# A two-layer decoder trunk on one core: the side sum of the expert rows moves from VectorE to ScalarE and GpSimd

## The reference, cut to what matters

```python
# per block of 128 tokens, 8 heads, 16 picks a head = 128 picks a token
e = ...                      # index of each pick in a table of 16384 experts
g = softmax(sc)              # gate of each pick
ue = u[e]; ve = v[e]         # two rows of 1024 floats a pick and token
a = gelu(einsum('thkd,td->thk', ue, xb)) * g
out = einsum('thk,thkd->td', a, ve)
```

## Time and profile before

| | |
|---|---|
| median of three runs | 2906.79 us |
| time of the profiled execution | 2907.78 us |
| its span in the trace | 2906.0 us |
| busy: TensorE matmul / VectorE / ScalarE / GpSimd | 78% / 75% / 41% / 43% |
| granted TensorE clock, mean | 0.921 of full speed |
| moved by DMA | 1170.26 MB, mean 403 GB/s |

### The profile page before, as it was taken

The page is one execution under the profiler, slowest core; times in us unless marked ns, Lnnn a source line. Parts: engine busy times, 40 slices in busy tenths (PEclk is TensorE's granted clock), DMA queues, the critical chain, the costliest instruction groups (busy, mean ns, idle before and its releaser), DMA issues.

```text
span 2906.0 us, 27009 instructions
## 1 busy us (share of the span) xinstructions
PE 2257.9 (78%) x7300; PEld 1200.6 (41%) x7300; DVE 2185.6 (75%) x5166; ACT 1183.3 (41%) x3457; POOL 1263.8 (43%) x1049
## 2 busy tenths in 40 slices
PE   8678777687877877787787878878778777876667
PEld 6535443354423544243343434433444434432222
DVE  2687768875878757796688876988679876887664
ACT  2144324343443433344444463445534453433333
POOL 0155335443454433444434543354434454345555
PEclk9799899999998998899898998999899998998989
DMA  6499999999999999999999999999999999999998
GB/s 270 174 410 421 413 359 420 421 420 413 404 420 422 420 389 415 421 422 421 421 391 416 422 421 421 388 413 421 421 418 398 420 421 420 404 420 422 421 422 351
DMA packets 170816, 1170.26 MB, mean 403 GB/s; under 512 B 19668, under 2 KB 19928, under 8 KB 36136
## 3 DMA queue, kind: packets, MB, share of 16 engines
q0 software_dynamic: 147456, 1073.81, 89.4%
q1 hardware_dynamic: 23208, 94.74, 8.3%
HBM read 1164.28 MB, written 4.19 MB: 402 GB/s over the span
## 4 chain that ended last, share of the span: by engine, by line
DMA 29%; DVE 14%; PE 10%; issue 6%; POOL 3%; ACT 3%; POOLq 0%; DVEq 0%; ACTq 0%
DMA ring<-in_uv,pick 27%; PE acc L1716 5%; DVE ring L1093 5%; POOL ring L666 3%; PE ps L1511 3%; DVE side L1084 1%; DMA xc<-h 1%; DMA stream<-in_strips 1%; ACT diag L1369 1%; DVE arena L968 1%; DVE arena L949 1%; DVE arena L950 1%; ACT coef L1361 1%; DVE arena L1039 1%; DVE arena L1043 1%
## 5 line engine op out<-in xcount | busy, mean ns | idle before, releaser
L666 POOL DMA_INDIRECT ring<-in_uv,pick x1024 | 1259.3, 1230 | 1616.5 <-PE acc L1716 1084.1
L1716 PE MATMUL acc<-ring,diag 128*128 128x512 f32 x2988 | 1523.6, 652 | 474.6 <-ACT diag L1369 474.1
L1093 DVE CUSTOM_DVE_ANT_0 ring<-ring,h_now 128x1024 f32<-128x1024 f32 x1024 | 1236.0, 1223 | 494.5 <-DMA ring<-in_uv,pick 483.2
L1716 PEld LDWEIGHTS acc<-ring,diag 128*128 128x128 f32 x2988 | 576.0, 204 | 1286.0 <-ACT diag L1369 719.4
L1358 ACT ACTIVATE gelu<-dots 128x1 f32<-128x1 f32 x1024 | 206.1, 201 | 1263.2 <-DVE dots L1093 1261.8
L1084 DVE SCALAR_TENSOR_TENSOR side<-ring,coef,side 128x1024 f32<-128x1024 f32 x270 | 346.1, 1282 | 18.9 <-ACT coef L1361 18.9
L1361 ACT ACTIVATE coef<-gate,gelu 128x1 f32<-128x1 f32 x1024 | 301.9, 295 | 33.2
L1369 ACT ACTIVATE diag<-ident,coef 128x128 f32<-128x128 f32 x747 | 300.1, 402 | 28.2 <-PE acc L1716 3.9
L1511 PE MATMUL ps<-resident,actT 128*128 128x256 f32 x896 | 217.5, 399 | 16.5 <-ACT actT L1170 16.5
L1511 PEld LDWEIGHTS ps<-resident,actT 128*128 128x128 f32 x896 | 175.7, 200 | 59.4 <-ACT actT L1170 18.1
L1478 PE MATMUL ps<-actT,stream 128*128 128x128 f32 x960 | 125.6, 292 | 27.4 <-DMA stream<-in_strips 26.6
(11 more groups left out here) (196 smaller groups left out, 1439.2 us busy)
## 6 DMA issues: line engine op xcount, KB each, us to landing
stream<-in_strips SPq DMA_DIRECT2D x102, 512.0 KB, 9.3
resident<-in_strips SPq DMA_DIRECT2D x18, 1024.0 KB, 12.3
ring<-in_uv,pick POOLq DMA_INDIRECT x1024, 14.9
ring<-in_strips SPq DMA_DIRECT2D x9, 1024.0 KB, 19.7
arena<-in_keys SPq DMA_DIRECT2D x8, 512.0 KB, 7.8
xc<-in_x SPq DMA_DIRECT2D x4, 512.0 KB, 6.2
h<-arena SPq DMA_DIRECT2D x4, 512.0 KB, 11.5
xc<-h SPq DMA_DIRECT2D x4, 512.0 KB, 7.8
```

The lines of the kernel that those rows point to most:

```text
L666: pool.indirect_dma_start(ring[:, n % SLOTS, :], None, tables[layer], bass.IndirectOffsetOnAxis(ap=pick[:, col:col + 1], axis=0),).then_in ...
L1093: dve.tensor_tensor_reduce(ring[:, slot, 0:D], ring[:, slot, 0:D], h_now[:], 1.0, 0.0, ALU.mult, ALU.add, dots[:, slot:slot + 1]).then_inc ...
L1716: m = pe.matmul(acc[:, b * 512:(b + 1) * 512], diag[:, turn % 4, :], ring[:, slot, D + b * 512:D + (b + 1) * 512], start=(r == 0 and i == ...
```

## The change

The table `VECTOR` becomes `ADDED`, with more even rounds: 25 picks in the first stage, 35 in each gla stage, 33 in each swa stage, 260 in all; 764 picks go to TensorE. VectorE's instruction L1084 is gone. For a listed pick ScalarE, after `coef`, multiplies the v half by it in place. GpSimd adds the product to `side`, right before the gather that will reuse the slot, which is nine picks later in its order. That addition marks the slot used, and so it now also gives the signal for the load of `xc`.

```diff
-VECTOR = {
-    "first": (
-        ((),) * 2 + ((4,),) + ((),) + ((1, 4, 7),) + ((0, 2, 4, 6),) + ((1, 3, 5, 7),) * 2 +
-        ((0, 2, 4, 6),) * 3 + ((1, 4, 7),) + ((2, 6),) + ((),) * 3),
-    "gla": (
-        ((1, 4, 7),) * 3 + ((0, 2, 4, 6),) + ((1, 4, 7),) * 2 + ((0, 2, 4, 6),) + ((1, 3, 5, 7),) +
-        ((0, 3, 6),) + ((2, 6),) + ((1, 4),) + ((2, 6),) + ((4,),) + ((),) * 3),
-    "swa": (
-        ((1, 4, 7),) * 2 + ((0, 2, 4, 6),) + ((0, 4),) + ((1, 5),) + ((0, 3, 6),) + ((2, 6),) +
-        ((1, 4, 7),) * 2 + ((2, 6),) + ((1, 3, 5, 7),) + ((0, 3, 6),) + ((),) * 4),
+ADDED = {
+    "first": ((),) * 3 + ((2, 6),) + ((1, 4, 7),) * 7 + ((2, 6),) + ((),) * 4,
+    "gla": ((1, 4, 7),) * 11 + ((2, 6),) + ((),) * 4,
+    "swa": ((1, 4, 7),) * 11 + ((),) * 5,
 }
...
+            def add(n):
+                s, at = divmod(n, PICKS)
+                r, i = divmod(at, BATCH)
+                added = ADDED[kind_of(s)]
+                pool.wait_ge(multiplied, ADDED_PICKS.index(n) + 1)
+                began = True
+                if i != added[r][0]:
+                    released(pool, pick_number(s, r, added[r][added[r].index(i) - 1]))
...
+                else:
+                    began = False
+                    pool.wait_ge(side_folded, s + 1)
+                slot = n % SLOTS
+                pool.tensor_tensor(side[:], ring[:, slot, D:2 * D], (side if began else xc)[:],
+                                   ALU.add).then_inc(used[slot], 1)
+
             def gathers(s, layer, begin, end):
                 for i in range(begin, end):
                     n = s * PICKS + i
+                    if n >= SLOTS and n - SLOTS not in TURN_OF:
+                        add(n - SLOTS)
                     if n >= SLOTS:
                         released(pool, n - SLOTS)
...
-                    dve.scalar_tensor_tensor(side[:], ring[:, slot, D:2 * D], coef[:, slot:slot + 1],
-                                             (side if began else xc)[:], ALU.mult, ALU.add).then_inc(used[slot], 1)
...
                         act.activation(coef[:, slot:slot + 1], gate[:, col:col + 1], ACT.Copy,
                                        scale=gelu[:, slot:slot + 1]).then_inc(weighed, 1)
+                        act.wait_ge(weighed, n + 1)
                         if i not in tensor[r]:
+                            v = ring[:, slot, D:2 * D]
+                            act.activation(v, v, ACT.Copy, scale=coef[:, slot:slot + 1]).then_inc(multiplied, 1)
                             continue
-                        act.wait_ge(weighed, n + 1)
```

More of the change, by code:

```diff
@@ L58 @@
 BEATS = PICKS // BEAT
-VECTOR = {
-    "first": (
-        ((),) * 2 + ((4,),) + ((),) + ((1, 4, 7),) + ((0, 2, 4, 6),) + ((1, 3, 5, 7),) * 2 +
-        ((0, 2, 4, 6),) * 3 + ((1, 4, 7),) + ((2, 6),) + ((),) * 3),
-    "gla": (
-        ((1, 4, 7),) * 3 + ((0, 2, 4, 6),) + ((1, 4, 7),) * 2 + ((0, 2, 4, 6),) + ((1, 3, 5, 7),) +
-        ((0, 3, 6),) + ((2, 6),) + ((1, 4),) + ((2, 6),) + ((4,),) + ((),) * 3),
-    "swa": (
-        ((1, 4, 7),) * 2 + ((0, 2, 4, 6),) + ((0, 4),) + ((1, 5),) + ((0, 3, 6),) + ((2, 6),) +
-        ((1, 4, 7),) * 2 + ((2, 6),) + ((1, 3, 5, 7),) + ((0, 3, 6),) + ((),) * 4),
+ADDED = {
+    "first": ((),) * 3 + ((2, 6),) + ((1, 4, 7),) * 7 + ((2, 6),) + ((),) * 4,
+    "gla": ((1, 4, 7),) * 11 + ((2, 6),) + ((),) * 4,
+    "swa": ((1, 4, 7),) * 11 + ((),) * 5,
 }
-TENSOR = {kind: tuple(tuple(i for i in range(BATCH) if i not in v) for v in of) for kind, of in VECTOR.items()}
+TENSOR = {kind: tuple(tuple(i for i in range(BATCH) if i not in v) for v in of) for kind, of in ADDED.items()}
 FOLD_AT = 14
@@ L86 @@
 TURN_OF = {n: turn for turn, n in enumerate(TURNED)}
+ADDED_PICKS = [n for n in range(STAGES * PICKS) if n not in TURN_OF]
 AT = {
@@ L304, in build @@
         weighed = sem("weighed")
+        multiplied = sem("multiplied")
         diag_ready = sem("diag_ready")
@@ L494, in load_block @@
                 elif stage:
-                    released(sp, pick_number(stage - 1, 0, VECTOR[kind_of(stage - 1)][0][0]))
+                    released(sp, pick_number(stage - 1, 0, ADDED[kind_of(stage - 1)][0][0]))
                 if prep.layer == 1:
@@ L652, in stage @@
                     gathers(s, layer, begin, (part + 1) * PICKS // PARTS)
+            def add(n):
[6 more added lines that the diff above has]
+                    released(pool, pick_number(s, r, added[r][added[r].index(i) - 1]))
+                elif any(added[:r]):
+                    last = max(m for m in range(r) if added[m])
+                    released(pool, pick_number(s, last, added[last][-1]))
+                elif kind_of(s) == "first":
+                    pool.wait_ge(side_begun, 1)
+                else:
[4 more added lines that the diff above has]
+                                   ALU.add).then_inc(used[slot], 1)
             def gathers(s, layer, begin, end):
@@ L1094, in part @@
                                                  ALU.add, dots[:, slot:slot + 1]).then_inc(dotted, 1)
[L1095 to L1098, removed]
                 return part
@@ L1707, in part @@
                     if r == FOLD_AT and picks[0] == 0:
-                        fold(s, VECTOR[kind_of(s)])
+                        fold(s, ADDED[kind_of(s)])
                     for i in picks:
```

## The result

The changed kernel takes 3037.69 us (median of four runs, 3022.35 to 3044.55) against 2906.26 us: ratio 1.0445, 95% interval 1.0417 to 1.0473. It is 131 us slower where 43 were forecast. The profiled execution took 3034.2 us, its span 3032.5 us.

What follows compares the result with a forecast made beforehand. The prediction took the DMA engines' pace as the bound. To the profiled 2907.8 us it added 24 for GpSimd's unrefilled lead and 19 for the late xc load, 2951, or 2950 against the median; range 2898 to 3050.

Steps and rivals of the forecast that it cites:

- The bound: Whole kernel: it runs at the pace of the DMA engines, 420 to 422 GB/s in most slices.
- the direction: Whole kernel: slower with chance 0.76, same 0.12, faster 0.12.
- GpSimd's work: GpSimd's rounds with three additions take 21.2 us against 21.1; lead not refilled, 24 us lost over four swa stages.
- VectorE's additions go: VectorE: 277 instructions, 355 us less; costed at nothing, since its time is mostly cover; ceiling 29 us.
- unless its dots are stretched: Sign on VectorE: it loses 355 us of busy time, unless its dots take longer.
- rival B: GpSimd becomes the bound: additions and dots block each other in turn, a round takes 23.9 us; 3075 us, chance 0.14.
- the placement: TensorE: 17 more picks and their new distribution over rounds, 35 us more work; costed at 0, upper end 6 us in four stages.
- the multiplication: ScalarE: 260 multiplications, 276 us more, between coef and the addition; hidden by the lead, costed at 0.
- The load of xc: Turns of stages 3 to 6: the load starts 5.8 us later, 19 us lost; stages 1 and 2 at 0.
- A: Only the xc load costs, as cheap additions let the lead be won back before round 5; 2926 us, chance 0.20.
- D: No change: GpSimd's additions are hidden by the 17.3 us of lead everywhere; 2907 us, chance 0.12.
- C: Faster: VectorE's dots come earlier in crowded rounds and slices below 420 GB/s partly fill; 2885 us, chance 0.12.

Runs made afterwards that it cites:

- one_after: Changed kernel, but the dot reads one input and writes no product back (a reduction of about the same length): 2960.5 us, ratio 1.0188.
- write: Changed kernel, but GpSimd writes zeros over the slot and half of the side sum in place of adding, about the same GpSimd time without reading: 2990.19 us, 1.0283.
- first: Changed kernel, but the first addition of stages 1 to 7, which signals the load of xc, stays on VectorE: 3018.63 us, 1.0394.
- short: Changed kernel, but GpSimd adds only 8 of 1024 columns, with all waits and the order kept: 2920.88 us, 1.0050.
- mult: Kernel before with the new table of picks and the multiplication on ScalarE, the addition still on VectorE: 2919.67 us, 1.0051.
- sqlate: Kernel before, but in stages 3 to 6 the norm of the next block begins three picks later: 2907.57 us, 1.0002.
- pick0: Kernel before, but the first addition of each stage from the second on is of pick 0 instead of pick 1: 2908.69 us, 1.0005.
- early: Changed kernel, but each addition stands one gather earlier in GpSimd's order: 3000.15 us, 1.0315.

## Why the prediction was wrong

*The bound, the direction and GpSimd's work: right.* The DMA's slices lost their 421 GB/s and the addition took 2.42 us (2.4 said). Of a round's eight gathers three stand behind an addition and its 0.81 us gap, five behind a 0.30 us gap, so a round of GpSimd's work is 8 x 1.18 + 5 x 0.30 + 3 x (0.02 + 2.42 + 0.81) = 20.7 us (21.2 said), against 21.1 for a round before and 22.7 for one after. That the sum came so near is partly luck: the gap behind an addition was 0.8 us, where I had put 0.3 for it and 0.3 for a wait for dots, and the additions hardly waited for dots (2.42 us, for 2.36 beside dots of one input).

*"VectorE's additions go ... I cost this at nothing": this step failed.* I had the exclusion from the earlier trace rows, but priced only in one direction, as a wait of GpSimd for dots. The other direction, a dot that waits up to 2.4 us for an addition, I noted as shown by no row and put at nothing; among the signs stood "unless its dots are stretched", but no term. In rival B too I put its price on the additions, which were hardly stretched. It stretched the dots by 330 us, a little less than the 355 us I counted as freed. By the runs with one-input dots the exclusion makes up 131 - 63 = 68 us. The 77 us between the changed kernel and one_after split, with write between them, into some 30 for gathers held up by dots and 48 for dots held up by additions, 10 of the 30 being there before the change. A plain lengthening of VectorE by as much gave 12 to 19. Why the blocked dots cost more than that is open: they fall on any pick that lands during an addition, the reductions on the added picks alone, but no run moved them.

*Without the exclusion, 63 us for a forecast of 43.* Of them 6 are the placement and 7 the multiplication, both costed at nothing. The other 50, the additions' time and the late load, are near to the 43. But they lie elsewhere: I set the gla stages at nothing because their xc comes in time, yet there too the queue is no longer refilled, and with all effects together stages 1 and 2 lost 28 us.

*The load of xc.* It starts 3.1 us later in stage 3 and 4.3 to 4.5 in stages 4 to 6 (5.8 said), ScalarE's four waits for it are 11.9 us on average (about 14 said), and first won 19 us (19 said), by the profiled executions in stages 3 to 6, where the sum had it. The place and the mechanism were right; that both figures are 19 is partly luck, since the delay was shorter and the medians are good to some 10 us. (The fullest queue of before was a little fuller than I said: the window from 2420 to 2430 has 18.1 us from issue to landing, not 17.3. That changes no term of the sum.) In the stage at 2335 the turn lost 10 us, but 5.5 are lost in first too; some 5 are left for the load, where I had 5.4. What a late load costs by itself is open: no run has the whole delay with short additions. The part of it that short has (14.2 us for mult's 12.6) costs nothing measurable, and easing the stall of before gained nothing in sqlate and pick0, so it seems to cost only while the additions keep the queue short.

*The rivals.* B, GpSimd as the bound (3075, 0.14), was nearer than the forecast, and its mechanism, mutual blocking, is half of what happened. But the blocking fell on the dots, a round of GpSimd's work fits into a round, and GpSimd still waits 641 us for TensorE. A and D fell with the interval, C with the sign. Nor was a gain hidden behind the exclusion: in short, where dots take 1.224 us and additions next to nothing, VectorE's waits for gathers grew to 795 us and the kernel was still 14 us slower than before; in write 840 us and 84 us. A rival that I had not named, TensorE's clock, gives no sign of being the cause, though no run separates it: the granted clock was 0.921 in the profiled execution before and 0.894 to 0.908 in the four after, and the four's fastest had 0.894; early, at 0.900, beat the one at 0.908 by 34 us.

## What to carry to other kernels

This kernel, at the pace of its DMA, lives on the lead of the engine that issues the transfers. Work given to that engine was cheap while it only ate surplus and dear beyond: 0.95 us an addition cost 17 us, twice that 117. And a gap that a timeline shows isn't yet time to be won: early took 173 us of gaps away, and held-up gathers and waits for ScalarE brought 224 back. Before moving work between VectorE and GpSimd, list both engines' instructions that read SBUF, and price the wait in both directions; what VectorE is relieved of may come back as stretched instructions that were never touched. And the time to recover from a stall belongs in the sum for every stage, not only for those in which a new stall is seen.

## What the runs showed of the hardware

- A GpSimd addition of two 128x1024 float32 operands takes 2.35 us alone (on average 2.36 beside one-input dots, 2.42 beside two-input dots).
- A two-input VectorE instruction issued during it stands until its end. The 178 dots that begin inside an addition all end 1.08 to 1.20 us behind it, and so do 33 that begin up to 0.65 us ahead of one; the stretched ones take 1.4 to 4.1 us for 1.22.
- The next gather starts 0.81 us behind an addition whose signal it waits for, 0.30 us behind another gather. Up to three small GpSimd writes of 0.11 us before a gather lengthen the spacing of two gathers by 0.04 us at most, and the gap behind an addition by 0.08.
- An indirect gather's instruction takes 0.94 us alone, 0.96 us on average beside one-input dots (one_after) and 1.17 to 1.30 us beside two-input dots.
